# MLP up and gate tiles of a float32 two-block transformer: 512-token matmuls replaced by seven block products of 256 tokens

## What is computed

```python
x = x + jnp.square(jax.nn.relu(h2 @ w_up[l])) @ w_down[l]        # first block

def swiglu(h, w_gate, w_up, w_down):
    return (jax.nn.silu(h @ w_gate) * (h @ w_up)) @ w_down
x = x + 0.5 * swiglu(rms_norm_2(x, ffn1_norm[l]), ...)           # before and after each mixer
```

## Time and profile before

| | |
|---|---|
| median of 3 runs | 2491.19 us (2490.41 to 2491.5) |
| profiled execution, first to last instruction | 2488.4 us |
| what lies around that span in a run | 2.8 us (median less span) |
| TensorE busy | 99% |
| VectorE, ScalarE, GpSimd busy | 50%, 39%, 8% |

### The profile page before, as it was taken

One profiled execution on the slowest core, in us unless ns is written; L12 is line 12 of the kernel. 1 busy time (PEld: TensorE's weight loads), 2 busy tenths in 40 slices (PEclk: granted clock), 3 DMA queues, 4 the chain that ended last, 5 costly groups with the idle time before them and its releaser, 6 DMA issues.

```text
span 2488.4 us, 27808 instructions
## 1 busy us (share of the span) xinstructions
PE 2471.6 (99%) x11236; PEld 2046.0 (82%) x11236; DVE 1235.0 (50%) x1674; ACT 961.9 (39%) x1415; POOL 198.7 (8%) x207
## 2 busy tenths in 40 slices
PE   9999999999999999999999999999999999999999
PEld 7878888888888888888888888888888888888887
DVE  7742554434474343466554444643444665544443
ACT  6677343322443232357432222422222575322223
POOL 2231010000020000012200000100000122000001
PEclk9999999999999999999999999999999999999999
DMA  7655433333233333245433332333332364333332
GB/s 212 141 129 124 136 102 103 95 100 101 85 94 101 102 93 95 86 134 143 119 94 102 93 101 86 102 95 100 93 102 81 123 142 129 94 102 93 102 91 79
DMA packets 79279, 267.40 MB, mean 107 GB/s; under 512 B 9904, under 2 KB 13232, under 8 KB 78768
## 3 DMA queue, kind: packets, MB, share of 16 engines
q1 hardware_dynamic: 69376, 233.57, 31.0%
q0 software_dynamic: 9776, 32.06, 6.4%
HBM read 234.56 MB, written 2.19 MB: 95 GB/s over the span
## 4 chain that ended last, share of the span: by engine, by line
PE 90%; DVE 3%; issue 2%; ACT 2%; POOL 1%; DMA 1%; SPq 0%; POOLq 0%; DVEq 0%; ACTq 0%
PE bank L845 29%; PE bank L847 29%; PE bank L846 29%; DVE w_lo L1237 1%; PE bank L861 1%; PE bank L876 1%; ACT w_hi L1006 1%; DVE x L1367 1%; PE bank L899 1%; ACT z L994 0%; PE bank L888 0%; PE bank L889 0%; ACT h_hi L1019 0%; POOL rel_bias L1561 0%; POOL square_sum L1542 0%
## 5 line engine op out<-in xcount | busy, mean ns | idle before, releaser
L845 PE MATMUL bank<-h_hi,w_hi 128*128 128x512 f32 x2224 | 872.4, 392 | 3.6 <-DVE w_lo L1237 1.5
L846 PE MATMUL bank<-h_lo,w_hi 128*128 128x512 f32 x2224 | 866.6, 390 | 0.0
L847 PE MATMUL bank<-h_hi,w_lo 128*128 128x512 f32 x2224 | 866.4, 390 | 0.0
L1237 DVE TENSOR_TENSOR w_lo<-w_raw,w_hi 128x1024 fp32r<-128x1024 f32 (+2 forms) x392 | 484.0, 1236 | 289.8 <-ACT w_hi L1006 288.6
L1006 ACT ACTIVATE w_hi<-w_raw 128x1024 fp32r<-128x1024 f32 (+1 forms) x435 | 449.1, 1034 | 398.7 <-PE bank L847 396.5
L845 PEld LDWEIGHTS bank<-h_hi,w_hi 128*128 128x128 f32 x2224 | 417.7, 188 | 88.0 <-DVE h_lo L1252 2.7
L847 PEld LDWEIGHTS bank<-h_hi,w_lo 128*128 128x128 f32 x2224 | 417.5, 188 | 88.0
L846 PEld LDWEIGHTS bank<-h_lo,w_hi 128*128 128x128 f32 x2224 | 417.9, 188 | 81.9 <-issue 0.5
L845 PE MATMUL bank<-act_hi,w_hi 128*128 128x512 f32 x960 | 373.6, 389 | 0.0
L846 PE MATMUL bank<-act_lo,w_hi 128*128 128x512 f32 x960 | 373.6, 389 | 0.0
L847 PE MATMUL bank<-act_hi,w_lo 128*128 128x512 f32 x960 | 373.6, 389 | 0.0
(11 more groups left out here) (203 smaller groups left out, 1724.8 us busy)
## 6 DMA issues: line engine op xcount, KB each, us to landing
w_raw<-ffn_wg_dram SPq DMA_DIRECT2D x88, 512.0 KB, 3.5
w_raw<-ffn_wu_dram SPq DMA_DIRECT2D x88, 512.0 KB, 3.5
w_raw<-w_in_dram SPq DMA_DIRECT2D x67, 512.0 KB, 3.6
w_raw<-ffn_wd_dram SPq DMA_DIRECT2D x64, 512.0 KB, 3.5
w_lo<-w_raw POOLq DMA_DIRECT2D x51, 512.0 KB, 4.5
w_raw<-w_up_dram SPq DMA_DIRECT2D x32, 512.0 KB, 3.5
w_raw<-w_down_dram SPq DMA_DIRECT2D x32, 512.0 KB, 3.7
w_raw<-w_out_dram SPq DMA_DIRECT2D x24, 512.0 KB, 3.6
```

The source lines that it names most:

```text
L845: engine.matmul(to, w_hi[s][:, lhs], hi, start=k == 0, stop=False)
L846: engine.matmul(to, w_hi[s][:, lhs], lo, start=False, stop=False)
L847: product = engine.matmul(to, w_lo[s][:, lhs], hi, start=False, stop=job == "k_last")
L1237: engine.tensor_tensor(lo, value, hi.bitcast(F32), ALU.subtract).then_inc(signals[event].s, 1)
```

## The change

The contraction (8 slices), the two output tiles of a pair and the two halves of the tokens are each halved, which makes a 2x2 by 2x2 block product, done with seven block products in place of eight (Winograd's form of Strassen's scheme). A **group** is one pair of up or gate tiles: seven products P1 to P7, each of four k-steps with 256 tokens, 84 matmuls. The five stages have 16 + 4·22 = 104 groups. What they need beside:

- Weights: a group's four blocks (512 floats per partition each) come in two loads of 512 KB (`s_load_a`, `s_load_b`) into one of two buffers. VectorE makes four sums of blocks (s_t13, two of them in one instruction of 1024, s_t2, s_t4), ScalarE the hi of all seven (three of 1024, one of 512), VectorE the lo of all seven, written over the raw ones. So loads for group g+2 wait for P6 and P3 of group g.
- Activations: for each pair of tiles the norm tile makes a full h on ScalarE first, then four mixtures of its quarters (three VectorE instructions of 512, 256 and 256), their hi on ScalarE (256 and 768) and lo on VectorE (256 and 768). The lo of the mixtures lies in the w_lo buffers, so that down and out weights have their lo written over w_raw, and the fetch of unit u+3 waits for the last matmul of unit u.
- Results: three partial results are copied out of PSUM by ScalarE (256 each: p1 behind P1, u1 behind P6, u3 behind P5), a fourth (p7 behind P7) as well; P6, P5, P3 and P4 wait for them. VectorE adds them (s_c22 of 256, s_sum of 512) and scales (s_gate or s_up: 512, 256, 256; the PSUM bank x of group g is free for group g+2 then). The first group of a stage has its own order, and the norm's sum, root and reciprocal lie in it, the reciprocal ahead of s_c22.
- Down: chunks of four tiles (a first one of two in the stages of width 2816). The eight results of a chunk are no longer made in one go: they become 32 steps that `fill` hands out, an equal share behind each group of the next chunk. Behind the groups of stage 1 stand 0, 0, 0 and then 16 steps each; in the others 0, 0, 0, then 4 each (four groups), then 8 each (fifteen groups). What is left at the end of the stage, 48 or 40 steps, runs in one go with the norm tiles in it.

```diff
+SLOT = HALF_K * P
+CHUNKS_FF = {FF1_TILES: (4,) * 8, FF2_TILES: (2, 4, 4, 4, 4, 4)}
+MLP_STAGES = (1, 2, 4, 5, 7)
+SPLIT_AFTER = 7
...
+B11, T1, T2, T4, B22, T3, B21 = range(7)
+B12 = T2
+PARTS = {"first": (B11, 2), "last": (B22, 2), "mixed": (T2, 2), "b21": (B21, 1)}
+PART_OF = {B11: "first", T1: "first", B22: "last", T3: "last", T2: "mixed", T4: "mixed", B21: "b21"}
+PRODUCTS = {"P1": (B11, "a11", "x"), "P2": (B21, "a12", "y"), "P3": (B22, "s4", "x"), "P4": (T4, "a22", "z"),
+            "P5": (T1, "s1", "x"), "P6": (T2, "s2", "x"), "P7": (T3, "s3", "z")}
+STEADY = ("P1", "P7", "P6", "P4", "P5", "P2", "P3")
+OPENING = ("P1", "P2", "P4", "P6", "P7", "P5", "P3")
+COPY_AFTER = {"P1": "p1", "P6": "u1", "P5": "u3"}
...
+        if s in MLP_STAGES and m % 2 == 1:
+            self.add("h_mix", (s, m // 2))
+            self.later(2, "h_mix_lo", s, m // 2)
...
+            if m < 2:
+                self.load("a", n + m)
+                self.load("b", n + m)
+            elif m == 2:
+                self.prepare_ahead(0)
...
+    def prepare(self, n, slots=8):
+        assert n == self.prepared
+        self.prepared += 1
+        for after, job, key in ((0, "s_t13", (n,)), (1, "s_t2", (n,)), (1, "s_hi", (n, "first")), (2, "s_t4", (n,)),
+                                (2, "s_hi", (n, "last")), (3, "s_lo", (n, "first")), (4, "s_hi", (n, "mixed")), (5, "s_lo", (n, "last")),
+                                (6, "s_hi", (n, "b21")), (7, "s_lo", (n, "mixed")), (9, "s_lo", (n, "b21"))):
+            self.later(slots + after, job, *key)
...
+    def fill(self, count):
+        for _ in range(min(count, len(self.filling))):
+            ms, n, source, size, k, last = self.filling.pop(0)
+            if k == 0:
+                self.filled = self.result(self.current, size, n * P, source)
+            self.steps(self.filled, [k], slots=False)
...
+    def strassen(self, g):
+        group = self.sg[g]
...
+        if self.prepared == g + 1 and g + 1 < self.block_end:
+            self.prepare(g + 1)
+        quota = self.quota
...
+        for name in group.order:
+            for k in range(HALF_K):
+                if k < HALF_K - 1:
+                    self.add("s_step", (g, name, k))
+                else:
+                    self.add("s_last", (g, name))
+                if k % 2 == 1:
+                    self.next_slot()
+            if name in COPY_AFTER:
+                self.add("s_copy", (g, COPY_AFTER[name]))
+            if name == ("P4" if group.opens else "P7"):
+                self.add("s_copy", (g, "q4" if group.opens else "p7"))
+            if name == "P5":
...
+                self.add("s_c22_open" if group.opens else "s_c22", g)
+            if name == ("P7" if group.opens else "P2"):
...
+                self.add("s_sum", g)
+            if name == "P6":
+                self.load("a", g + 2)
+                if group.opens:
+                    self.norm(self.pending_norm)
+                    self.pending_norm = None
+        self.load("b", g + 2)
+        self.fill(quota)
+        self.grouped()
+    def grouped(self):
+        if self.waiting:
+            self.filling += self.waiting
+            self.waiting = []
+            self.quota = -(-len(self.filling) // self.quota_over)
...
+    def hidden_pair(self, s, pair):
...
+            self.strassen(g)
+            self.later(1, "s_relu", g)
+            self.later(3, "s_square", g)
+            self.groups_done += 1
+        else:
+            self.strassen(g)
+            self.later(1, "s_gate", g)
+            self.later(3, "s_silu", g)
+            self.later(6, "s_rescale", g)
+            self.strassen(g + 1)
+            self.later(1, "s_up", g + 1)
+            self.groups_done += 2
+        self.group_of[s, pair] = self.groups_done - 1
+        self.later(5 if s == 1 else 3, "s_act", s, pair)
+        self.later(7 if s == 1 else 5, "s_act_lo", s, pair)
...
+        self.split_job = "split_late"
+        start = 0
+        chunks = chunk_units(n_tiles)
+        self.quota = 0
+        for c, (start, size, units) in enumerate(chunks):
+            last = c == len(chunks) - 1
+            for pair in range(start // 2, (start + size) // 2):
+                self.hidden_pair(s, pair)
+            self.waiting = [(ms, n, ("act", s, start), size, k, last) for ms in units for n in range(len(ms)) for k in range(size)]
+            self.quota_over = 1 if last else chunks[c + 1][1] // 2 * (1 if s == 1 else 2)
+        self.filling += self.waiting
+        self.waiting = []
+        self.prepare_ahead(4)
+        self.fill(len(self.filling))
+        self.split_job = "split_v"
+        self.h_last[s] = ("s_mm", (self.groups_done - 1, "P3"))
         self.pending_norm = s + 1
...
+    def prepare_ahead(self, slots):
+        while self.prepared <= self.groups_done + 1 and self.prepared < self.block_end:
+            self.prepare(self.prepared, slots)
+            slots += 14
...
+                    if k == 0:
+                        pe.wait_ge(*done("s_lo", (g, PART_OF[slot])))
...
+                        if name in COPY_BEFORE:
+                            pe.wait_ge(*done("s_copied", (g, COPY_BEFORE[name])))
+                        if name == ("P7" if group.opens else "P4"):
+                            pe.wait_ge(*done("s_copied", (g, "q4" if group.opens else "p7")))
...
+                    engine.matmul(to, slot_hi[:, g % 2, slot, lhs], hi, start=opens, stop=False, skip_group_check=True)
+                    engine.matmul(to, slot_hi[:, g % 2, slot, lhs], lo, start=False, stop=False, skip_group_check=True)
+                    product = engine.matmul(to, slot_lo[:, g % 2, slot, lhs], hi, start=False, stop=closes, skip_group_check=True)
...
+                    if m >= 2:
+                        act.wait_ge(*done("mix_4", (s, m // 2 - 1)))
+                        act.wait_ge(*done("h_lo", (s, m - 2)))
+                    engine.activation(h_full[:, m % 2, :], x[:, m, :], ACT.Copy, scale=h_gain(s, m)).then_inc(signals["h_full"].s, 1)
+                    plain = first_half if m % 2 == 0 else slice(0, TOKENS)
+                    engine.activation(h_hi[:, m, plain], x[:, m, plain], ACT.Copy, scale=h_gain(s, m)).then_inc(signals["h_hi"].s, 1)
+                elif job == "h_mix":
+                    s, j = key
+                    act.wait_ge(*done("mix_31", key))
+                    engine.activation(h_hi[:, 2 * j, second_half], h_mixed[:, 0, :], ACT.Copy)
+                    act.wait_ge(*done("mix_4", key))
+                    engine.activation(hs_hi[:, :, j, :], h_mixed[:, 1:4, :], ACT.Copy).then_inc(signals["mix_hi"].s, 1)
...
+                elif job == "s_copy":
+                    g, what = key
+                    product = {"p1": "P1", "u1": "P6", "u3": "P5", "p7": "P7", "q4": "P4"}[what]
+                    act.wait_ge(*done("s_mm", (g, product)))
...
+                elif job == "s_silu":
+                    z1, z2 = zs_of(key)
+                    act.wait_ge(*done("s_out", key))
+                    engine.activation(z1[:, :], z1[:, :], ACT.Silu)
+                    engine.activation(z2[:, :], z2[:, :], ACT.Silu).then_inc(signals["silued"].s, 1)
...
+                elif job == "h_mix":
+                    s, j = key
+                    v.wait_ge(*done("h_full", (s, 2 * j + 1)))
+                    if j > 0:
+                        v.wait_ge(*done("mix_hi", (s, j - 1)))
+                    engine.tensor_tensor(h_mixed[:, 0:2, :], h_quarters[:, 0:4:3, :], h_quarters[:, 1:2, :].broadcast_to([P, 2, HALF]),
+                                         ALU.subtract).then_inc(signals["mix_31"].s, 1)
+                    v.wait_ge(*done("mix_31", key))
+                    engine.scalar_tensor_tensor(h_mixed[:, 2, :], h_quarters[:, 0, :], -1.0, h_mixed[:, 1, :],
+                                                ALU.mult, ALU.subtract).then_inc(signals["mix_2"].s, 1)
+                    v.wait_ge(*done("mix_2", key))
+                    engine.scalar_tensor_tensor(h_mixed[:, 3, :], h_mixed[:, 2, :], -1.0, h_quarters[:, 2, :],
+                                                ALU.mult, ALU.subtract).then_inc(signals["mix_4"].s, 1)
+                elif job == "h_mix_lo":
+                    s, j = key
+                    v.wait_ge(*done("mix_hi", key))
+                    engine.tensor_tensor(h_lo[:, 2 * j, second_half], h_mixed[:, 0, :], h_hi[:, 2 * j, second_half].bitcast(F32), ALU.subtract)
+                    rest(hs_lo[:, :, j, :], h_mixed[:, 1:4, :], hs_hi[:, :, j, :], "mix_lo")
+                elif job == "s_t13":
+                    n = key
+                    v.wait_ge(a_landed[n % 2].s, 16 * (n // 2 + 1))
+                    v.wait_ge(b_landed[n % 2].s, 16 * (n // 2 + 1))
+                    if n >= 2:
+                        v.wait_ge(*done("s_mm", (n - 2, "P5")))
+                        v.wait_ge(*done("s_mm", (n - 2, "P7")))
```

(32 more changed lines are left out.)

451 lines of the change are left out of this document (318 added, 133 removed).

## The result

The changed kernel takes **2614.14 us** (median of 4 runs, 2610.96 to 2617.49) against 2491.35 for the kernel before beside it: a ratio of 1.0495, 95% interval 1.0481 to 1.0510. The forecast was 2514 us, with a range of 2425 to 2578. The direction was right; the size was not: the loss is 123 us where 23 were forecast, and the time lies above the range.

The account below looks back on a forecast made before the run. TensorE, busy 2471.6 of 2488.4 us, was taken as the bound. Its saving of 127 us against added waits of 45 (stage starts), 54 (out projections) and 51 (MLP to MLP) gave +23 on 2491.2: 2514 us, range 2425 to 2578.

Parts of the forecast that it names:

- TensorE's part: All 104 groups: 8736 matmuls of 256 columns at 0.115 us replace 4992 of 512 at 0.2267; 127 us less.
- Transitions and openings: Stage edges: VectorE's lateness adds 54 us at three out projections, 51 from MLP to MLP, 33 in opening groups.
- The clock: Idle stretches at transitions: a granted clock below full would add to them; no size given.
- Ordinary groups: Groups after a stage's opening: no wait with 8 or 16 down steps, 0.72 us each with 4; 12 us in all.
- rival 2: Ordinary groups: cross-engine waits make each of 73 groups 0.7 us late, +51, 2565 us; chance 0.08.
- at nothing: Loads throughout: issued a group or more ahead, landing in 3.5 us, so they cost no time.
- Signs named ahead: Profile after: what it would show if the forecast were right, such as VectorE above 75% busy, or wrong.
- rival 1: Whole kernel: TensorE stays the bound, VectorE's waits are half of 150 us, spacing 0.1133; 2424 us; chance 0.39.
- rival 3: All groups: weight loads of 0.189 us cannot hide behind matmuls of 0.115; +519, about 3030 us; chance 0.02.

Follow-up runs that it names:

- thin_all: Changed kernel with the weights' preparation, the later stages' mixtures and GpSimd's sums all cut to 8 columns (output not the reference's); 2521.27 us.
- rest_between: Changed kernel, but in the out projections VectorE computes the former unit's weights' lo between the residual and the norm tile; 2580.52 us.
- thin_sums: Changed kernel with GpSimd's additions of squares for the MLP stages' norms on 8 columns of 512; 2591.18 us.
- early_p1: Best version found, plus each opening group computing P1 of the second group ahead of its own P2's last step; 2559.88 us.
- one_ahead: Changed kernel with one group's weights prepared ahead of a stage in place of two; 2625.58 us.
- filled: Reordered kernel (weights' lo after residual, GpSimd's sums behind mixtures; 2575.92 us) plus 48 or 24 unread matmuls before P2's last step in opening groups; 2578.38 us.

## Why the prediction was wrong in size

**TensorE's part: mis-sized, 44 us.** "I take 0.115 since both steps together give it": the change's matmuls stand 0.120 apart, outside the upper end of 0.118 too, and the saving is 83 us, not 127. Two steps in a row were too short to read a price from that counts 8736 times: the timeline rounds each start to 0.01 us, and 0.005 us more a matmul is 44 us. The earlier trace rows alone hold the clue: 226.7 ns at 512 columns is 13.3 above 512/2.4, and a fixed part doesn't halve. I set the N/2.4 + 2.5 of the Trainium skill ("TensorE: Matmul & The Clock Gate", Back-to-back issue gap) beside my figure and did not put the trace's own remainder into that form: 106.7 + 13.3 = 120.0.

**Transitions and openings: right cause, mis-sized, some 38 us.** Forecast for them 138 (54 + 51 + 33 for the first groups and the norm), measured 175.9. They are VectorE's, as forecast, and "the waits are its cause as much as the work" holds: `thin_all` leaves 101 us of them with most of the work gone, and `rest_between` makes the kernel 34 us faster by order alone. Two things were missing in the sum:
- GpSimd's additions. I took 1.52 for 1.22 from the earlier trace rows and charged it ahead of stage 2 alone. At the mixtures an addition costs VectorE 1.07 us each time, in all five stages, and `thin_sums` prices that at 23 us.
- What stands ahead of the last tiles' answers. I set the out projection's end against the fourth product's last step. At stages 1, 4 and 7 TensorE already stops at the first product's last step, 9.3 us for h_lo of tile 6, then 2.6 us at the second's for tile 7 and 1.4 to 2.7 for the next answer. VectorE's order set most of the first wait (`rest_between`, 1.5 us in its place ahead of stage 4); `early_p1` and `one_ahead` only moved waits.

How the 38 us are shared between the two is not shown.

**The clock: named, not priced.** From 1330 to 1334 us, behind the waits at stage 4's opening, the granted clock is 0.52 and the matmuls stand 0.213 us apart, not 0.120: half the clock (1.2 GHz for 2.4). By such spacing matmuls at half the clock cost 37.7 us of the 229 (239 starts of 256 columns 0.195 to 0.225 apart, 75 of 512 at 0.41 to 0.44), 3.7 before. They lie within the waits counted above. Whether the time would be shorter without them is open: `filled` gave 5.5 us of it back without a gain, but put in more work than the wait held.

**Ordinary groups.** With 8 down steps: "no wait there" is right, all of them wait 0.0, and rival 2 fell. With 4 steps I said 0.72; 14 of 16 wait 0.5 to 0.6, the others 0.9 and 1.7. With 16 steps I said none and it was 1.28 in each of 12, 15 us. The path was the one I had named, silu ahead of the copy p7 ahead of P4, with 0.3 us to spare; what I left out is that ScalarE first waits for a load:

```profile
488.49 1.06 ACT L1245 ACTIVATE w_hi<-w_raw 128x1024 fp32r<-128x1024 f32 x1 [8.04 <-DMA w_raw<-w_down_dram]
490.95 1.22 DVE L1526 TENSOR_TENSOR w_raw_lo<-w_raw,w_hi 128x1024 fp32r<-128x1024 f32 x1
...
494.53 0.37 ACT L1305 ACTIVATE part_b<-bank 128x256 f32<-128x256 f32 x1
...
494.95 0.19 PEld L1085 LDWEIGHTS bank<-h_hi,slot_hi 128*128 128x128 f32 x1 [0.61 <-ACT part_b L1305]
```

The load was issued at 484.83 and ScalarE's copy starts as it lands, so `w_raw_lo` comes just ahead of the scaling, the scaling is late, and silu and p7 behind it. I had put loads "at nothing", with slack from the fetch to the use by TensorE; the first user is ScalarE's queue, seven slots behind the fetch.

**Sum of the errors**: 44 + 38 + 13 (groups: 25.3 for 12) + 4 (start and mixers) = 99, and 2514 + 99 = 2613, one less than measured.

**Signs named ahead.** VectorE above 75% was off (72%). Full TensorE in groups with 8 steps was right, in those with 16 wrong. P4 waits for the copy p7 in the groups behind the first of a stage, as said (0.9 to 1.4 us). I had said 16 to 20 us at each out projection and some 25 at each MLP-to-MLP edge: it is 13 to 14 in the former and 21 to 25 in the opening behind it, and 36 and 28 at the edges with their openings. TensorE above 97% did not come, so rival 1 fell; rival 3 did too, with loads recorded at 0.195 us behind matmuls 0.120 apart; its 3030 should have read 3010 (2491 + 519).

## What to carry to other kernels

Splitting matmuls to save work multiplies their fixed part: take it from the old spacing (spacing less columns over the clock), not from a pair of starts. Where a change saves on the bound engine all along, but loads the others at the edges, sum the edges first: here 83 us saved along 104 groups stand against 204 of added waits, some 175 of them at the stages' edges, and even with most of the added work thinned out the edges cost more (101) than was saved. There, follow each queue in order and put what is ready ahead of what waits for an answer: a change of order gave 34 us.

## What was unexpected of the hardware

- This kernel's matmuls have a fixed 13.3 ns each beside their columns, and at 192 and 128 columns alike they cost some 111 ns. At 256 columns the same weights 32 times running were no quicker than new ones (120 ns).
- A GpSimd addition that reads and writes the on-chip memory holds up a VectorE instruction with two such inputs that starts behind it, until it ends: 16 elements took 1.25 us beside it, 512 took 1.77, and 0.69 without. Moved, it held up the next such instruction instead (0.42 to 0.96 us). The Trainium skill, "SBUF — State Buffer", section "SBUF: two separate sides", says this: the two engines share a port pair as an exclusive lock, held for a whole instruction, which VectorE's instructions with two inputs there need as well. The trace agrees: in the odd tile above the addition ends at 1290.80 and the mixture, begun at 1289.60, ends 0.55 us later, about its own length. A subtraction of 1024 elements beside one lost only 0.3 us, which had looked like a small slowdown; it had begun when the addition had 0.44 us left.
- TensorE's granted clock was 0.67 over the 26 us in which it was busy for 12.3, behind a wait of 9.3 us, and 1.00 in mid-stage.
